# Mixer A's norm: the reciprocal root by three GpSimd powers instead of a logarithm and three exponentials on ScalarE

## The reference

```
def diff_attention(q1, q2, k1, k2, v, lam, lam_init, subln_g):
...
    of = o.astype(jnp.float32)
    of = of * lax.rsqrt(jnp.mean(jnp.square(of), -1, keepdims=True) + RMS_EPS)
    of = of * subln_g.astype(jnp.float32) * (1.0 - lam_init)
    return of.reshape(B, T, -1).astype(v.dtype)
```

## Time and profile before

| what | value |
|---|---|
| median of 3 runs | 1358.97 us |
| lowest and highest | 1357.38 and 1359.63 us |
| the profiled execution, its own time | 1355.7 us |
| its span in the trace | 1353.9 us |
| TensorE busy (share of the span) | 1283.0 us (95%) |
| VectorE busy | 714.9 us (53%) |
| GpSimd busy | 538.1 us (40%) |
| ScalarE busy | 486.1 us (36%) |
| mean granted TensorE clock | 0.968 |

### The profile page before, as it was taken

One profiled execution on the slowest core, in us unless ns is written; L12 is line 12 of the kernel. 1 busy time (PEld: TensorE's weight loads), 2 busy tenths in 40 slices (PEclk: granted clock), 3 DMA queues, 4 the chain that ended last, 5 costly groups with the idle time before them and its releaser, 6 DMA issues.

```text
span 1353.9 us, 17426 instructions
## 1 busy us (share of the span) xinstructions
PE 1283.0 (95%) x6898; PEld 1056.6 (78%) x6898; DVE 714.9 (53%) x1107; ACT 486.1 (36%) x1016; POOL 538.1 (40%) x290
## 2 busy tenths in 40 slices
PE   7999789998999999999989979989989999999996
PEld 6998555688888888888889966556888888888885
DVE  4234786627865062360485177874387642624506
ACT  4334568623222122221232346674233222322221
POOL 4443710042644444444354445100445444444444
PEclk9999889998999999999989988899989999999998
DMA  7432100031433232322144320000314323322311
GB/s 249 118 105 65 45 1 1 2 109 47 142 102 100 93 94 99 102 94 91 40 116 120 109 78 1 1 1 1 125 49 154 93 93 97 106 93 94 94 62 62
DMA packets 66657, 110.07 MB, mean 81 GB/s; under 512 B 14928, under 2 KB 27536, under 8 KB 66448
## 3 DMA queue, kind: packets, MB, share of 16 engines
q1 hardware_dynamic: 65424, 104.76, 24.3%
q10 hardware_dynamic: 1152, 4.19, 0.9%
HBM read 106.85 MB, written 2.10 MB: 80 GB/s over the span
## 4 chain that ended last, share of the span: by engine, by line
PE 86%; DVE 9%; ACT 2%; POOL 1%; issue 1%; DMA 1%; SPq 0%; POOLq 0%; ACTq 0%; DVEq 0%
PE ps L624 16%; PE ps L626 16%; PE ps L625 16%; PE ps L620 9%; PE ps L621 9%; PE ps L622 9%; PE ps L683 3%; PE ps L675 3%; DVE probs_a L1232 2%; PE ps L719 2%; DVE negmax L1189 2%; PE ps L579 1%; DVE xres L1099 1%; DVE probs_a L1234 1%; DMA raw<-in_w_in 1%
## 5 line engine op out<-in xcount | busy, mean ns | idle before, releaser
L487 POOL TENSOR_TENSOR w_lo<-raw,w_hi 128x1024 fp32r<-128x1024 f32 (+2 forms) x192 | 460.3, 2403 | 711.9 <-ACT w_hi L875 711.9
L875 ACT ACTIVATE w_hi<-raw 128x1024 fp32r<-128x1024 f32 (+2 forms) x192 | 196.4, 1026 | 617.4 <-PE ps L626 389.1
L620 PE MATMUL ps<-xt_hi,w_lo 128*128 128x512 f32 (+1 forms) x576 | 213.3, 370 | 8.8 <-DVE xt_lo L1080 8.8
L621 PE MATMUL ps<-xt_hi,w_hi 128*128 128x512 f32 (+1 forms) x576 | 212.6, 369 | 0.0
L622 PE MATMUL ps<-xt_lo,w_hi 128*128 128x512 f32 (+1 forms) x576 | 212.6, 369 | 0.0
L624 PE MATMUL ps<-w_hi,mt_lo 128*128 128x512 f32 x384 | 150.4, 392 | 0.0
L626 PE MATMUL ps<-w_lo,mt_hi 128*128 128x512 f32 x384 | 149.5, 389 | 0.0
L625 PE MATMUL ps<-w_hi,mt_hi 128*128 128x512 f32 x384 | 149.4, 389 | 0.0
L624 PE MATMUL ps<-w_hi,xt_lo 128*128 128x430 f32 (+1 forms) x384 | 138.0, 359 | 6.4 <-DVE xt_lo L1080 4.5
L626 PE MATMUL ps<-w_lo,xt_hi 128*128 128x430 f32 (+1 forms) x384 | 137.1, 357 | 0.0
L625 PE MATMUL ps<-w_hi,xt_hi 128*128 128x430 f32 (+1 forms) x384 | 137.1, 357 | 0.0
(11 more groups left out here) (159 smaller groups left out, 1922.9 us busy)
## 6 DMA issues: line engine op xcount, KB each, us to landing
raw<-in_w_up SPq DMA_DIRECT2D x64, 512.0 KB, 3.3
raw<-in_w_down SPq DMA_DIRECT2D x64, 512.0 KB, 3.7
raw<-in_w_in SPq DMA_DIRECT2D x40, 430.0 KB, 3.4
raw<-in_w_out SPq DMA_DIRECT2D x8, 512.0 KB, 3.7
raw<-in_w_in SPq DMA_DIRECT2D x8, 428.0 KB, 3.3
raw<-in_w_out SPq DMA_DIRECT2D x12, 256.0 KB, 3.7
xres<-in_x SPq DMA_DIRECT2D x4, 512.0 KB, 6.4
rows<-in_ln_g ACTq DMA_DIRECT2D x4, 512.0 KB, 4.5
```

Of the source, the lines that this page charges most:

```text
L487: nc.gpsimd.tensor_tensor(unit_of(w_lo, u), unit_of(raw, u), unit_of(w_hi, u).bitcast(F32), ALU.subtract).then_inc(s_lo_ready, 1)
L620: mm(o, wl[:, c], a_hi[:, k, cols], start=first, stop=False)
L621: mm(o, wh[:, c], a_hi[:, k, cols], start=False, stop=False)
L875: A(unit_of(w_hi, u), unit_of(raw, u), ACT.Copy).then_inc(s_hi_ready, 1)
```

## The change

ScalarE's logarithm and its three exponentials in each layer are taken out. GpSimd raises each of the three tiles to the power -0.5 in place, with one instruction of 128x512 each, and raises `rms_ready` in ScalarE's stead. Each power waits only for VectorE's emptying of its own square sums. They stand in GpSimd's program behind the two multiplications of the compressed scores and ahead of the weights' `split`. Everything else is as it was: the same instructions on TensorE, VectorE and the DMA queues, in the same order.

```diff
@@ -70,6 +70,7 @@
         11: ("cmp_scores", 1), 12: ("square_sums", 0), 16: ("cmp_turn", 0), 17: ("cmp_turn", 1),
         18: ("square_sums", 1), 19: ("pool", 0), 20: ("pool", 1), 21: ("square_sums", 2)}
+SQUARE_SUMS = [step for step in SIDE if SIDE[step][0] == "square_sums"]
 SIDE_NUMBER = {step: n for n, step in enumerate(SIDE)}
@@ -548,6 +549,10 @@
                 link(nc.gpsimd.tensor_tensor(cv, cv, cm, ALU.mult))
                 nc.gpsimd.tensor_tensor(cmp_s[:], cmp_s[:], over24(3), ALU.mult).then_inc(s_cmp_probs, 1)
 
+                for c in range(3):
+                    pool.wait_ge(s_side_emptied, nth("side_emptied", layer, SIDE_NUMBER[SQUARE_SUMS[c]] + 1))
+                    nc.gpsimd.tensor_tensor(rms[:, c], rms[:, c], kc[:, K_HALF:K_HALF + 1].to_broadcast([P, SEQ]), ALU.pow) \
+                        .then_inc(s_rms_ready, 1)
                 split(layer, U_OUT + RING, U_MLP + 2)
                 rstd_of(layer, 0)
@@ -1016,14 +1021,6 @@
 
                         act.wait_ge(s_side_emptied, nth("side_emptied", layer, SIDE_NUMBER[t - 2] + 1))
                         A(mt_hi[:, 3 + t - 21], pooled[:, t - 21], ACT.Copy).then_inc(s_pool_hi, 1)
-                    if t == 23:
-
-                        act.wait_ge(s_side_emptied, nth("side_emptied", layer, len(SIDE)))
-                        flat = rms[:].rearrange("p a q -> p (a q)")
-                        A(flat, flat, ACT.Ln).then_inc(s_chain_act, 1)
-                    if 24 <= t <= 26:
-                        act.wait_ge(s_chain_act, layer + 1)
-                        A(rms[:, t - 24], rms[:, t - 24], ACT.Exp, scale=-0.5).then_inc(s_rms_ready, 1)
                     if 26 <= t <= 28:
                         act.wait_ge(s_oa_normed, nth("oa_normed", layer, t - 25))
                         A(mt_hi[:, t - 26], oa[:, t - 26], ACT.Copy).then_inc(s_oa_hi, 1)
```

## The result

The changed kernel takes 1759.7 us (median of 4 runs, 1758.5 to 1761.0) against 1358.2 us before in the same session: a ratio of 1.297, 95% interval 1.295 to 1.299, or 401.5 us more. It is slower, as forecast, and the time lies inside the range, but the forecast was 113 us more, and the sum behind it described another mechanism than the one that the trace shows.

What follows compares the result with a forecast made beforehand. The stage was taken as bound by a loop through all four engines, at step 23 by ScalarE. Per layer 56 - 4.6 + 5.1 = 56.5 us, 113 us for two, gave 1472 us; 8-in-10 range 1349 to 1850 us.

Steps and rivals of the forecast that it cites:

- The logarithm's gap: Around step 23 of both layers: TensorE idle 2.9 us behind ScalarE's logarithm, plus 1.7 us lost to slow clock.
- T: Time of one 128x512 power on GpSimd, not in the trace; taken as 20 us, 39 ns a column.
- second rival: Attention stage: VectorE not held during powers, only the wait for roots counts; 1387 us at T = 20; chance 0.26.
- 6T - 7: Forecast's added us for both layers: VectorE held by three powers a layer, less the gain, plus slow clock; 113 us.
- 3T - 4: Us lost per layer while three powers hold up VectorE's factor and scaling; 56 us with T = 20.
- the general rule: GpSimd and two-SBUF-input VectorE instructions share ports; the first holds them for its whole instruction; given 6 in 10.
- the row of the same operation: One-column power, 311.64 to 312.19 us; VectorE's two-input instruction beside it kept its usual 0.43 us.
- The port is not held: Rival: one column may be read at once and the port let go; T over 15 us, 1360 to about 2100; chance 0.26.
- 3T - 46 us: Loss per layer over T = 15: third root ready at 194.1 + 3T against 240.2; 14 us at T = 20.
- covered under 28 us a power: GpSimd's weights' split behind the powers stands idle 86.58 us before 280.68, covering three powers under 28 us each.

## Why the prediction was right or wrong

**What bounds the stage, and the gain: right.** The logarithm's gap was priced at 4.6 us a layer, 9.2 in all, from TensorE's idle 2.9 us and its slow clock behind them. With powers of 64 columns, too short to matter, 8.7 us are gained (9.3 in the stretches of the traces); the two single runs with short powers give 7.6 and 7.8.

**The length of a power: mis-sized.** T was taken as 20 us between bounds of 1.3 and 230, from their geometric middle and a little above. It is 82, and this is the larger step that failed: with the port free, the prediction's own second rival gives 28 us more at T = 20, and 399 at the measured T. The working stopped at "no row tells" whether the 0.29 us by which a one-column power exceeds a plain instruction are paid once or by column. A little over half of them, 0.159 us, are paid by column. The bounds did their duty and the middle did not: when one row of the very operation stands at one end and a row of another operation at the other, the middle between them is a coin. Taking the one-column excess as the cost of a column, 0.29 x 512 = 148 us, would have been nearer in ratio than 20, and would have put the forecast too high, at 6T - 7 = 881 us more.

**The port: wrong.** The forecast let a power hold VectorE up for its length, three times a layer, 3T - 4. A power costs VectorE 0.8 us at its start: VectorE's 0.16 us at 200.29 stand 6.6 us into a power of 82. The plain multiplications of the earlier trace rows do hold VectorE up to about their end. The Trainium skill, page "SBUF — State Buffer", section "Who interferes with whom", says that a VectorE instruction with two SBUF inputs contends with a GpSimd instruction that reads SBUF, and calls the shared port pair an exclusive lock. The trace agrees in that they contend (3.23 us in place of 2.45). Where the section adds, of VectorE's modes that use two ports, that whoever issues first has the pair for the whole instruction, and the prediction took it for every pair of instructions, the measurement decides against it for a power. I gave the general rule 6 in 10 and the row of the same operation 4. That row, was weaker than the prediction made it: by the rule its VectorE instruction would have ended near 312.6 (312.19 and its 0.43 us) and it ended at 312.23, so it did speak against the rule, but at one column even a power's hold is too short to be seen (0.04 us at 64 columns), and it could not say how the hold grows.

**The rival that came true.** "The port is not held" put the loss at 3T - 46 us a layer from the moment GpSimd is free and the moment VectorE wants the last root. With T = 81.9 that is 199.7 us, 399.4 for two, against 199.6 measured to the third root. With what the stage loses behind the third root, 1.85 us in layer 0 and 1.69 in layer 1, it comes to 402.9, where the span grew by 402.8. It had 0.26, of which T above 60 us was only 0.4 x 0.30 = 0.12.

**The range: in part luck.** Its upper end, 1850 us, is T = 83 with the port held and T = 97 without. The forecast's own formula at the measured T gives 485 us more, 1844 us, where 1759.7 are measured. The time lies inside because the range was as wide as the doubt about T, not because its centre or its mechanism was right.

**The clock: a small term, too large.** 1.7 us for each of three waits were charged a layer. Measured are 1.85 us in layer 0 and 1.69 in layer 1, all behind the last, the slow clock's part not told apart from the rest of the stage there: while GpSimd's next power runs, TensorE's slow clock after the first two costs nothing, since what follows waits for that power anyway.

**The work behind.** GpSimd's weights were covered under 28 us a power. At 82 they start 201 us later, but so does TensorE's need for them: 42.3 us of waiting in front of them are left, of 86.6 before, and they are not late.

## What to carry to other kernels

Before work moves to an idle engine, price its operation at full size by a row of that operation, and if there is only a small one, take the excess over a plain instruction as a cost of each column until a run says otherwise (here 148 us for 82; the middle of the bounds gave 20). An off-path engine gives only as much cover as lies between the release of its first input and the use of its last output (here 46 us for three instructions), whatever its share of busy time. And where a reduction's result is repeated over partitions, do the costly function on the small form and repeat it afterwards.

## What the runs showed of the hardware

A power on GpSimd takes 0.39 us and 0.159 us a column from 1 to 512 columns, within some 0.5 us of that line, and the same on 64 as on 128 partitions, with the exponent 0.8 as with -0.5, with a constant base as with the mean squares (the last three at 64 columns); a multiplication of 128x512 takes 1.27 us. A long power holds up VectorE's two-input instructions only at its start: 0.04 us at 64 columns, 0.19 at 160, 0.78 at 512, the last as much as a multiplication of 512 columns does, and nothing in the rest of its 82 us. That fits an instruction that reads its operand first and then works without the port; what it does inside was not measured.
